# A two-layer decoder step on one core: the second layer's last three expert slots added to stored rows by DMA, and two slots' rows given to the next layer by one-hot products

## The chip, the cores and the metric

One NeuronCore of a Trainium2 chip. The metric is the device time of one execution in microseconds; the time before is the median of three runs. All positions in time below are microseconds from the start of the one profiled execution.

## The reference, cut to what matters

Two layers run over 512 prompt tokens and 64 sample tokens of width 1024. A layer adds a mixer (chunk MLP and differential attention) to x and then a mixture of experts, in which each token goes to the two best experts of its best group (4 groups of 4 experts):

```
def hier_moe(x, g2, r_g, r_e, w_gate, w_up, w_down):
    h = rmsnorm(x, g2).reshape(b * t, d)
    pg = softmax(h @ r_g);  gi = argmax(pg);  gw = max(pg)
    le_sel = (h @ r_e).reshape(-1, 4, 4)[:, gi]
    tw, ti = top_k(softmax(le_sel), 2);  tw = tw / sum(tw)
    gates = one_hot(gi * 4 + ti) * gw * tw
    a = silu(h @ w_gate) * (h @ w_up) * gates
    return a @ w_down          # summed over the experts

for l in range(2):
    x = x + merge_out(...)     # mixer
    x = x + hier_moe(x, ...)
```

The outputs are x of both token groups, and keys, values and normalised rows of each layer.

## The kernel before, in words

Tokens stand in five tiles of 128 rows (four of the prompt, one with the 64 sample rows, whose number is TP = 4); x is held in SBUF, [128, 5, 1024]. Each engine has its own program written out by hand, and semaphores with names order them: `full[u]` and `read[u]` say that a PSUM bank u was written or read, `landed` that a weight piece is there, `x_ready` that a tile of x is done.

The experts of a layer run as 13 slots of 128 rows (`SLOTS`, line 86); a slot belongs to one expert or is shared by two or three, and the experts are ordered by size while the kernel runs. For slot n POOL gathers rows by an indirect DMA, PE turns them, multiplies them with gate and up weights (`up`), turns the activations (`turn_act`) and multiplies with the down weights (`down`); ACT copies the result from PSUM to `y_sb` (`result`, line 1473), and POOL scatters its 128 rows into the DRAM tensor `y_rows` (`scatter`, line 651). A token has two rows there: its upper choice in the first 640 rows, its lower choice in the last 640. A choice of one of a group's first three experts lands in either half; the fourth experts (positions 12 to 15, slots 9 to 12) are always an upper choice. `LAST` is slot 10, the first slot whose first position is 12 or above; slots 10, 11 and 12 are the last three.

Weights come in pieces of 1 MB that SP issues in a fixed order (line 494) as buffers come free. In the second layer the third piece waits until the first layer's last upper rows have been loaded (`high_in`, line 470).

The end of a layer is this. When slots 8 and 9 have been scattered, ACT loads the lower rows of all tiles (line 1499), and DVE adds them to x with their gates behind the last slot's product (`add_low`, line 2127). After the last copy ACT waits for all scatters and loads the upper rows of all tiles (`load_high`, line 1535). DVE adds them tile by tile (lines 2186 to 2205). At the seam between the layers, tile 0 is added in two halves, and PE turns each half as soon as it is there (`turn_input`, line 757); until then PE runs 39 dummy products (`keep_busy`, line 755). In the second layer SP stores each tile when it is added (line 512), and the kernel ends when the stores have landed. Rows beyond the slots' capacity would go to extra slots (`extras`); the given input needs none.

Indices for the gather and scatter are products of one-hot matrices with row numbers (`index_rows`, line 1152; `index` on DVE, line 2006). At the start POOL writes zeros into the lower half of `y_rows` (line 571).

## Time and profile before

| what | value |
|---|---|
| median of 3 runs | 958.11 us (956.31 to 962.84) |
| profiled execution, its span | 959.0 us (no other time of it is given) |
| PE busy | 924.7 us, 96% |
| DVE, ACT, POOL busy | 396.8, 245.8, 190.9 us |
| DMA moved | 197.51 MB, 206 GB/s over the span |

Busy times are sums over the whole span; what a stage waits for is seen only in its own stretch. Two stretches matter here: the seam between the layers (about 460 to 490) and the tail (from 920 on). In a timeline row, the first number is the start, the second the duration (for several instructions in one row, from the first start to the last end), and what stands in brackets is the idle time before and what ended it. L715 and L713 are the lines of PE's helper, so all its products share them; a 128x128 by 512 product in f32 is two records. L656 is POOL's scatter; its duration is the time on POOL, and the rows land later.

### The profile page before, as it was taken

The page shows a single profiled execution, that of the slowest core. Times are in us where ns is not written, and L with a number is a line of the kernel's source. Part 1 is how long each engine was busy: PE and PEld are TensorE (multiplying, and loading weights), DVE is VectorE, ACT ScalarE, POOL GpSimd, SP SyncE. Part 2 cuts the span into 40 slices and gives each one's busy share as a digit, 9 for nine tenths or more (in the row PEclk, how much of TensorE's full clock was granted, in tenths as well). Part 3 has the DMA queues.
Part 4 walks back from the last instruction along what each step waited for, and adds up shares of the span by engine and source line. Part 5 has one row for each costly group of instructions (what it writes and reads, how often), then busy time and mean ns, then how long its engine had stood idle before and what let it go on. Part 6 is the DMA issues. An engine that isn't in the chain of part 4 may idle for free. (4 is left out here: it accounts for less than half of the span.)

```text
span 959.0 us, 13967 instructions
## 1 busy us (share of the span) xinstructions
PE 924.7 (96%) x5140; PEld 448.3 (47%) x5140; DVE 396.8 (41%) x1007; ACT 245.8 (26%) x493; POOL 190.9 (20%) x263
## 2 busy tenths in 40 slices
PE   9999999999999999999999999999999999999991
PEld 6444445556546443334544344455564464333330
DVE  2403225667547663111333122456764774511123
ACT  3211256552111021111131113765320012211110
POOL 2233201331200111111134032023220011111100
PEclk9999999999999999999999999999999999999996
DMA  9716003351017899998772150134210279999966
GB/s 334 290 46 273 2 1 138 89 176 45 23 45 265 319 410 399 401 403 352 263 268 65 36 239 1 55 109 156 84 45 22 114 267 411 414 386 403 423 236 231
DMA packets 39197, 197.51 MB, mean 206 GB/s; under 512 B 7096, under 2 KB 7224, under 8 KB 23248
## 3 DMA queue, kind: packets, MB, share of 16 engines
q1 hardware_dynamic: 19456, 136.03, 35.7%
q0 software_dynamic: 15312, 45.72, 13.8%
q10 hardware_dynamic: 4352, 14.76, 4.3%
q8 instruction: 45, 0.74, 0.3%
q14 instruction: 32, 0.26, 0.1%
HBM read 176.20 MB, written 28.84 MB: 214 GB/s over the span
## 5 line engine op out<-in xcount | busy, mean ns | idle before, releaser
L715 PE MATMUL ps<-ring,hT 128*128 128x512 f32 (+3 forms) x1312 | 397.1, 584 | 1.0 <-ACT ring L1406 0.6
L715 PEld LDWEIGHTS ps<-ring,hT 128*128 128x128 f32 (+2 forms) x1312 | 150.5, 152 | 197.2 <-issue 193.6
L715 PE MATMUL ps<-ring,cat 128*128 128x512 f32 (+2 forms) x560 | 181.8, 598 | 0.0
L715 PEld LDWEIGHTS ps<-ring,cat 128*128 128x128 f32 (+2 forms) x560 | 65.7, 157 | 81.0 <-issue 79.3
L2119 DVE TENSOR_TENSOR hT<-ps,par 128x512 f32<-128x512 f32 x52 | 33.7, 686 | 154.4 <-PE ps L713 149.4
L656 POOL DMA_INDIRECT y_rows<-hn,isca x26 | 27.0, 1039 | 230.7 <-ACT hn L1484 226.9
L535 POOL TENSOR_TENSOR st<-st,half 128x1 f32<-128x1 f32 (+3 forms) x60 | 63.5, 1058 | 11.0 <-POOL st L533 10.8
L533 POOL TENSOR_SCALAR st<-st 128x1 f32<-128x1 f32 (+3 forms) x60 | 16.0, 266 | 228.8 <-DVE st L1594 83.1
L1594 DVE TENSOR_REDUCE st<-sqj 128x8 f32<-128x512 f32 x20 | 13.5, 682 | 111.5 <-ACT sqj L1318 111.4
L715 PE MATMUL ps<-hT,ring 128*128 128x512 f32 x128 | 57.1, 599 | 0.7 <-DVE tmp L1651 0.7
L1484 ACT COPY hn<-ps 128x1024 f32<-128x1024 f32 x24 | 24.3, 1012 | 95.4 <-PE ps L715 95.4
L715 PE MATMUL ps<-kva,hT 128*32 128x512 f32 (+1 forms) x128 | 43.7, 596 | 0.0
L541 POOL DMA_DIRECT2D kc<-in_ck x32 | 24.6, 768 | 95.0 <-PE ps L715 71.7
L1390 ACT ACTIVATE ring<-ps,st 128x128 f32<-128x128 f32 (+3 forms) x64 | 33.2, 524 | 27.7 <-DVE st L1718 27.6
L1318 ACT ACTIVATE sqj<-ps,st 128x512 f32<-128x512 f32 (+1 forms) x20 | 13.7, 686 | 96.7 <-PE ps L715 90.1
L715 PEld LDWEIGHTS ps<-hT,ring 128*128 128x128 f32 x128 | 23.7, 190 | 29.9 <-issue 28.4
L648 POOL DMA_INDIRECT hT<-h_rows,igat x24 | 25.4, 1057 | 50.9 <-DVE isca L2017 45.4
L541 POOL DMA_DIRECT2D vc<-in_cv x32 | 17.6, 550 | 87.8 <-PE ps L715 71.9
L1467 ACT ACTIVATE cat<-ps 128x256 f32<-128x256 f32 x26 | 10.0, 384 | 96.9 <-PE ps L715 96.9
L1573 DVE TENSOR_TENSOR hT<-ps,g_sb 128x512 f32<-128x512 f32 x20 | 13.0, 688 | 48.6 <-PE ps L713 48.4
L715 PE MATMUL ps<-v,hT 128*32 128x512 f32 (+2 forms) x96 | 29.1, 596 | 1.8 <-SPq L167 1.8
L715 PE MATMUL ps<-kc,cat 128*32 128x512 f32 (+1 forms) x128 | 29.4, 596 | 0.0
(278 smaller groups left out, 1136.4 us busy)
## 6 DMA issues: line engine op xcount, KB each, us to landing
ring<-in_w SPq DMA_DIRECT2D x84, 1024.0 KB, 10.7
kc<-in_w SPq DMA_DIRECT2D x10, 1024.0 KB
vc<-in_w SPq DMA_DIRECT2D x10, 1024.0 KB
v<-in_w SPq DMA_DIRECT2D x10, 1024.0 KB
kva<-in_w SPq DMA_DIRECT2D x10, 1024.0 KB
kc<-in_ck POOLq DMA_DIRECT2D x32, 256.0 KB, 3.7
vc<-in_cv POOLq DMA_DIRECT2D x32, 256.0 KB, 3.3
h_rows<-qk ACTq DMA_DIRECT2D x10, 512.0 KB, 2.6
```

The lines of the kernel that those rows point to most:

```text
L533: nc.gpsimd.tensor_scalar(stat["ms"][at, 0:n], src, 1.0 / size, EPS, ALU.mult, ALU.add).then_inc(*pool_c.inc())
L535: nc.gpsimd.tensor_tensor(dst, stat["ms"][at, 0:n], half[at, 0:n], ALU.pow).then_inc(*pool_c.inc(*label))
L541: pool.dma_start(buffer(b % 2, g), view(d[table][bass.DynSlice(l * NPOOL + page, 1)])).then_inc(*arrived[b % 2].inc("kv", b, by=16))
L648: pool.indirect_dma_start(hs[:, b, :], None, h_rows, bass.IndirectOffsetOnAxis(index, 0), bounds_check=TOK - 1, oob_is_err=False).then_inc ...
L656: pool.indirect_dma_start(rows, bass.IndirectOffsetOnAxis(index, 0), y_sb[:, b, :], None, bounds_check=rows.shape[0] - 1, oob_is_err=False ...
L715: ins = pe.matmul(out, lhsT, rhs, start=start, stop=stop, skip_group_check=loose)
L1318: nc.scalar.activation(sqj[at, t % 2, :], bank(u)[at, :], ACT.Square, scale=stat["rs"][at, t:t + 1]).then_inc(*act_s.inc("sq", name, t))
L1390: ins = nc.scalar.activation(e_sb[:, n % 2, m, 0:(i + 1) * P], bank(f"S{n % 2}", m)[:, 0:(i + 1) * P], ACT.Exp, bias=stat["nb"][:, c:c + 1 ...
L1484: nc.scalar.copy(y_sb[:, b, :], ps[:, 6:8, :].rearrange("p a n -> p (a n)")).then_inc(*read["O"].inc("down", *key))
L1573: vec.tensor_tensor(hT[:, hf * HALF:(hf + 1) * HALF, t * P:(t + 1) * P], bank(f"T{hf}").rearrange("p (j t) -> p j t", j=HALF), g, ALU.mult ...
L1594: vec.tensor_reduce(stat["ssk"][:, 8 * t:8 * t + 8], groups(sqj[:, t % 2, :], 8, DK), AX.X, ALU.add).then_inc(*dve_s.inc("ss" + name, t))
L2119: vec.tensor_tensor(hsT[:, b, hf * HALF:(hf + 1) * HALF, :], bank(f"T{hf}").rearrange("p (j t) -> p j t", j=HALF), g, ALU.mult).then_inc(* ...
```

## The change

It does two things.

**Second layer.** The lower rows and the upper rows of slots 0 to 9 are loaded by SP together (`y_low` and `y_soon`), when slots 8 and 9 have been scattered. DVE adds both (`add_low`, `add_soon`): tiles 0 to 2 after the product of slot 11, tiles 3 and 4 after that of slot 12. SP stores each tile at once, into one output tensor `y`, which has three times 128 rows more than tokens. For slots 10, 11 and 12 PE and DVE make each row's gate (`slot_gates`, at slots 8 and 9; parts prepared in `direct_gates`), ACT multiplies it in when it copies the result, and POOL adds the 128 rows to `y` in DRAM by an indirect DMA with addition; rows of a slot that hold no token go to one of the additional rows. POOL's first such DMA waits until all five stores have landed.

**Seam.** When slot 10 has been scattered, ACT loads tile 0's upper rows (`first_rows`) before it copies the result of slot 11, and DVE adds them. The results of slots 11 and 12 are kept in SBUF (`y_kept`), and PE multiplies them with two one-hot matrices (`token_hot`) to get what tile 0 still lacks, in two halves, each two products; DVE adds the halves from PSUM. POOL scatters slots 11 and 12 only after `first_rows` has landed; ACT then loads the upper rows of tiles 1 to 4. The 39 dummy products become 4 before the four products and 2 behind them.

Besides, POOL writes one more blank of 128 rows at the start, and DVE computes `direct_gates` at slot 6 in both layers.

```diff
+        DIRECT = range(LAST, NSLOT)
+        GATES_AT = 8
+        y_soon = [ring[:, c, i * D:(i + 1) * D] for c in (1, 4) for i in range(2)] + [first_rows]
+        y_last = ring[:, 0, 0:D]
+        CARRIED = range(NSLOT - 2, NSLOT)
+        y_kept = [ring[:, 4, i * D:(i + 1) * D] for i in range(2)]
+        token_hot = [oS[:, 0:P], oS[:, 3 * P:4 * P]]
...
@@ SP
                         sp.wait_ge(*high_in[TP].at("high"))
+                        sp.wait_ge(*full["S1"].at("carried", 1))
...
+                if l == L - 1:
+                    for b in range(2):
+                        sp.wait_ge(*y_out[b].at("y", "m", last_slot(b, LAST)))
+                    for t in range(NT):
+                        sp.dma_start(y_low[0:n, t, :], y_rows[TOK + at:TOK + at + n, :])...
+                        sp.dma_start(y_soon[t][0:n, :], y_rows[at:at + n, :])...
+                    for t in range(NT):
+                        sp.wait_ge(x_ready.sem, L * NT + t + 1)
+                        sp.dma_start(d["y"][at:at + n, :], x[0:n, t, :]).then_inc(*stored.inc(by=16))
...
-            for t in range(NT):
-                n = NROW if t == TP else P
-                sp.wait_ge(x_ready.sem, L * NT + t + 1)
-                sp.dma_start(d["ys"] if t == TP else d["yp"][t * P:(t + 1) * P, :], x[0:n, t, :]).then_inc(*stored.inc(by=16))
             sp.wait_ge(stored.sem, stored.now())
+            for b in range(2):
+                sp.wait_ge(*y_out[b].at("y", "m", last_slot(b)))
...
@@ POOL
+                    pool.dma_start(y_rows[0:P, :], blank).then_inc(*blank_out.inc(by=16))
...
+                    if l == L - 1 and key[0] == "m" and key[1] in DIRECT:
+                        wait(stored.sem, NT * 16)
+                        j = DIRECT.index(key[1])
+                        src = y_last if key[1] == NSLOT - 1 else y_sb[:, b, :]
+                        pool.indirect_dma_start(d["y"], bass.IndirectOffsetOnAxis(iadd[:, j:j + 1], 0), src, None,
+                                                bounds_check=d["y"].shape[0] - 1, oob_is_err=True, compute_op=ALU.add)...
+                        return
+                    if l < L - 1 and key == ("m", CARRIED[0]):
+                        wait(*soon_first.at("soon"))
...
@@ PE
-                    keep_busy(39, "I")
+                    keep_busy(2, "I")
...
-                        pe.wait_ge(*dve_s.at("half"))
+                        pe.wait_ge(*read["S0"].at("carried", 0))
...
+                def slot_gates():
+                    pe.wait_ge(*dve_s.at("gate_parts"))
+                    claim("I")
+                    for j, s in enumerate(DIRECT):
+                        for t in range(NT):
+                            mm(bank("I")[:, j * 4:j * 4 + 3], onehot[:, s % 4, t, :], gate_parts[:, t, 0:3], ...)
...
+                if l < L - 1:
+                    keep_busy(4, "T0")
+                    pe.wait_ge(*dve_s.at("token_hot"))
+                    for c in range(2):
+                        u = f"S{c}"
+                        claim(u)
+                        for j, s in enumerate(CARRIED):
+                            if j == 0:
+                                pe.wait_ge(*read["O"].at("down", "m", s))
+                            else:
+                                pe.wait_ge(*read["JI"[c]].at("down", "m", s))
+                            mm(bank(u), token_hot[j], y_kept[j][:, c * W:(c + 1) * W], start=(j == 0), stop=(j == 1), ...)
...
@@ ACT
-                    if n == LAST + 1:
+                    if n == LAST + 1 and l < L - 1:
...
+                    if n == NSLOT - 1 and l < L - 1:
+                        act.wait_ge(*y_out[(CARRIED[0] - 1) % 2].at("y", "m", CARRIED[0] - 1))
+                        act.wait_ge(*y_out[(CARRIED[0] - 2) % 2].at("y", "m", CARRIED[0] - 2))
+                        act.dma_start(first_rows, y_rows[0:P, :]).then_inc(*soon_first.inc("soon", by=16))
                     if n >= 1:
                         result((n - 1) % 2, ("m", n - 1), n >= 3)
...
-                    for t in range(NT):
+                    for t in range(1, NT):
                         high_load(t)
...
@@ DVE
                     gated(n % 2, ("m", n))
+                    elif n >= LAST + 1:
+                        for t in (range(3) if n == LAST + 1 else range(3, NT)):
+                            add_low(t)
+                            add_soon(t)
...
+                    dve.wait_ge(*soon_first.at("soon"))
+                    link(vec.scalar_tensor_tensor(x[:, 0, :], first_rows, stat["soon"][:, 0:1], x[:, 0, :], ALU.mult, ALU.add))
...
+                            dve.wait_ge(*full[f"S{hf}"].at("carried", hf))
+                            vec.scalar_tensor_tensor(x[:, 0, cols], bank(f"S{hf}"), stat["gAB"][:, 0:1], x[:, 0, cols], ALU.mult, ALU.add)...
```

## Rows read from the trace of the kernel before

**Rows 1.** The page: span, and busy time of the engines.
```profile
span 959.0 us, 13967 instructions
PE 924.7 (96%) x5140; PEld 448.3 (47%) x5140; DVE 396.8 (41%) x1007; ACT 245.8 (26%) x493; POOL 190.9 (20%) x263
```

**Rows 2.** Windows of 10 us: stretch, length, busy time per engine, clock, DMA share, GB/s.
```profile
460.00:470.00 10.00, 8.62 (x54) 3.68 (x46) 6.75 (x6) 2.57 (x5) 2.69 (x2) 1.00 0.57 209
...
940.00:950.00 10.00, 0.00 (x0) 0.00 (x0) 2.57 (x2) 0.00 (x0) 0.34 (x1) 0.56 0.75 254
```

**Rows 3.** The chain of waits in the tail: start, us, what.
```profile
937.92 0.59 ACT hn L1482
...
939.36 3.51 DMA y_rows<-hn,isca
...
952.55 1.28 DVE x L2125
```

**Rows 4.** Timeline of PE at the seam.
```profile
468.79 9.21 PE L731 MATMUL ps<-c 128*128 128x128 f32 x78 [1.38 <-ACT hn L1482]
477.84 1.21 PE L713 MATMUL ps<-c,x 128*128 128x128 f32 x8
479.27 5.39 PE L715 MATMUL ps<-ring,hT 128*128 128x512 f32 x12 [0.22 <-issue]
484.50 1.04 PE L713 MATMUL ps<-c,x 128*128 128x128 f32 x8
```

**Rows 5.** Timeline of ACT, POOL and DVE at the seam.
```profile
463.74 1.01 ACT L1484 COPY hn<-ps 128x1024 f32<-128x1024 f32 x1 [1.51 <-PE ps L715]
...
466.61 0.58 ACT L1480 COPY hn<-ps 128x512 f32<-128x512 f32 x1 [1.85 <-DMA y_rows<-hn,isca]
...
469.00 0.98 POOL L656 DMA_INDIRECT y_rows<-hn,isca  x1 [1.57 <-issue]
...
472.97 2.58 ACTq L1517 DMA_DIRECT2D cat<-y_rows  x5
...
476.92 1.42 DVE L2195 SCALAR_TENSOR_TENSOR x<-cat,st,x 128x512 f32<-128x512 f32 x2 [8.67 <-DMA cat<-y_rows]
```

**Rows 6.** Timeline of the second layer's last slot and of the tail.
```profile
919.76 2.98 ACTq L1499 DMA_DIRECT2D qk<-y_rows  x5
...
930.97 6.55 DVE L2125 SCALAR_TENSOR_TENSOR x<-qk,st,x 128x1024 f32<-128x1024 f32 x5
...
931.96 0.44 PE L713 MATMUL ps<-c,cat 128*128 128x128 f32 x2
...
942.89 2.27 ACTq L1517 DMA_DIRECT2D cat<-y_rows  x5
...
946.26 2.61 DVE L2125 SCALAR_TENSOR_TENSOR x<-cat,st,x 128x1024 f32<-128x1024 f32 x2 [8.74 <-DMA cat<-y_rows]
...
955.05 0.53 SPq L512 DMA_DIRECT2D out_ys<-x  x1
```

**Rows 7.** Windows chosen for their DMA rate and clock, columns as in rows 2.
```profile
38.00:42.00 4.00, 3.38 (x18) 2.04 (x17) 3.33 (x10) 1.17 (x2) 0.36 (x1) 1.00 0.08 31
...
453.00:465.00 12.00, 12.00 (x55) 4.36 (x54) 4.19 (x4) 3.15 (x5) 0.98 (x1) 1.00 0.97 368
...
938.00:941.00 3.00, 0.00 (x0) 0.00 (x0) 0.00 (x0) 0.50 (x1) 0.98 (x1) 1.00 0.25 94
941.00:942.00 1.00, 0.00 (x0) 0.00 (x0) 0.00 (x0) 0.00 (x0) 0.00 (x0) 0.65 0.98 397
```

**Rows 8.** Second layer: index products, PE's wait, and DVE at slot 7.
```profile
L715 PE MATMUL ps<-rows_of,cat 128*128 128x4 bf16 x30 | 1.6, 166 | 0.0
...
PE ps L715 <- SPq L167: 1.8, 1, 1.8
...
857.42 1.29 DVE L2119 TENSOR_TENSOR hT<-ps,par 128x512 f32<-128x512 f32 x2 [10.27 <-PE ps L713]
```

**Rows 9.** DMA issues: line, count, KB each, median us from issue to landing.
```profile
out_ys<-x SPq DMA_DIRECT2D x1, 256.0 KB, 3.5
c<-in_c ACTq DMA_DIRECT2D x1, 64.0 KB, 1.9
```

More of the change, by code:

```diff
@@ L700, in first_extras, with add_sums @@
                     only_if(pool, n_extra > 1, lambda: first_extra(1), uncounted=hs_inx)
-                extras(pool, n_extra, move, start=first_extras, uncounted=[*hs_inx, *y_outx])
+                def add_sums():
+                    for b in range(2):
+                        wait(*y_out[b].at("y", "m", last_slot(b)))
+                    for t in range(NT):
+                        n, at = NROW if t == TP else P, PLACE[t] * P
+                        wait(*summed.at("sum", t))
+                        pool.dma_start(d["y"][at:at + n, :], x[0:n, t, :], accum_op=ALU.add).then_inc(*topped.inc("added", by=16))
+                extras(pool, n_extra, move, start=first_extras, done=add_sums if l == L - 1 else None, uncounted=[*hs_inx, *y_outx])
         ATT = [(i, h) for i in range(TP) for h in range(H)]
@@ L1166, in index_rows @@
                                    start=(t == 0), stop=(t == NT - 1), inc=full[u].inc("idx", g) if ends and at.stop == P else None)
+                def slot_gates():
+                    pe.wait_ge(*dve_s.at("gate_parts"))
+                    claim("I")
+                    for j, s in enumerate(DIRECT):
+                        for t in range(NT):
+                            mm(bank("I")[:, j * 4:j * 4 + 3], onehot[:, s % 4, t, :], gate_parts[:, t, 0:3], start=(t == 0), stop=(t == NT - 1),
+                               inc=full["I"].inc("gates") if (s == NSLOT - 1 and t == NT - 1) else None)
                 def turn_in(b, key, arrival):
@@ L2016, in index @@
                     dve.wait_ge(*read[u].at("idx", g))
+                    for s in GROUPS[g]:
+                        if l < L - 1 and s in CARRIED:
+                            vec.tensor_scalar(stat["row"][:, CARRIED.index(s):CARRIED.index(s) + 1], work[:, s - s0:s - s0 + 1], SKIP + 1.0, None, ALU.add)
+                        if l == L - 1 and s in DIRECT:
+                            vec.tensor_scalar(iadd[:, DIRECT.index(s):DIRECT.index(s) + 1], work[:, s - s0:s - s0 + 1], SKIP, c32[:, C_SINK][:, DIRECT.index(s):DIRECT.index(s) + 1], ALU.add, ALU.min)
                     vec.tensor_scalar(isca[:, s0:s0 + n], work[:, 4:4 + n], SKIP, None, ALU.add).then_inc(*dve_s.inc("idx", g))
@@ L2115, in in_turned, with slot_gates @@
+                def slot_gates():
+                    dve.wait_ge(*full["I"].at("gates"))
+                    n = len(DIRECT)
+                    vec.tensor_reduce(stat["hand"][:, 0:n], bank("I")[:, 0:4 * n].rearrange("p (s c) -> p s c", c=4)[:, :, 0:3], AX.X, ALU.add).then_inc(*read["I"].inc("gates"))
                 def in_turned(b, key, halves=(0, 1)):
@@ L2158, in _ @@
                         late_gates()
+                    if n == 6:
+                        direct_gates()
+                    if n == GATES_AT + 1 and l == L - 1:
+                        slot_gates()
                     if n in INDEX_AT:
@@ L2172, in slot, with sum_late @@
                     gated(b, (key, b))
+                def sum_late():
+                    dve.wait_ge(stored.sem, NT * 16)
+                    for t in range(NT):
+                        n = NROW if t == TP else P
+                        dve.wait_ge(*low_in[t].at("low"))
+                        dve.wait_ge(*high_in[t].at("high"))
+                        link(vec.tensor_scalar(x[0:n, t, :], y_low[0:n, t, :], stat["late"][0:n, t:t + 1], None, ALU.mult))
+                        vec.scalar_tensor_tensor(x[0:n, t, :], y_high[0:n, t, :], stat["rest"][0:n, t:t + 1], x[0:n, t, :], ALU.mult, ALU.add).then_inc(*summed.inc("sum", t))
                 def add_late():
@@ L2182, in extra_index @@
                         index(g)
-                extras(dve, n_extra, slot, done=add_late, start=extra_index)
+                extras(dve, n_extra, slot, done=add_late if l < L - 1 else sum_late, start=extra_index)
                 def add_high(t):
```

141 lines of the change are left out of this document (106 added, 35 removed).

## The prediction

> **What bounds the kernel now.** I read the page first: PE is busy 924.7 of 959.0 us [rows 1], so only two places can give much: where PE stands still, and where it does work that is none. The windows show both [rows 2]. From 460 to 470 PE is busy 8.62 of 10 us and then runs dummy products; from 940 on it does nothing, while DMA is at 0.75. The chain of waits gives the order of that tail [rows 3]: ACT copies the last slot's result (937.92), POOL scatters it into y_rows (939.36, landed 3.51 later); five loads bring all upper rows back from 942.89, DVE adds them, and x is stored until 958.55 (issue 955.05 [rows 6] plus 3.5 to landing [rows 9]). So 20.5 us pass after the last copy, all of it one DMA waiting for another. The timeline of the seam shows the same chain once more [rows 4, 5]: copy, scatter, load of tile 0 (issue 472.97), DVE's addition at 476.92, first product of the next layer at 479.27. The 9.21 us of dummies at 468.79 lie inside this wait. The granted clock is 1.00 throughout until PE stops.
>
> All times below are on the clock of the profiled execution. The page gives no time for it beside the span, 959.0, which is 0.9 above the median of the runs; 0.9 is taken off at the end.
>
> **Seam, step by step.** Tile 0 gets the rows of slots 0 to 10 by a load (first_rows) and those of slots 11 and 12 by one-hot products from SBUF.
> - ACT now waits for the scatter of slot 10 before result(11). That landing ended a wait at 466.6 in the trace [rows 5], and before it held only the last slot's copy. Issue of first_rows 0.5 (five issues took 2.58), result(11) 1.01, two half copies of 0.58: done at 468.1, 468.7 and 469.3. Before, result(11) stood at 463.74, so ACT is late, but nobody on PE asks yet: PE itself resumed only at 468.79, 1.38 after its last instruction.
> - PE: a dummy is 9.21/39 = 0.236, so 4 take 0.9 and end at 469.7. A product of 128x128 by 512 is two records of 5.39/12 = 0.45 [rows 4], so 0.9; four take 3.6, to 473.3, each after its copy. Two dummies more: 473.8. From the turn of tile 0 to the first product took 1.43 (477.84 to 479.27): 475.2. That is 4.0 earlier.
> - DVE: first_rows (512 KB) is bounded by 3.5 (a transfer of 256 KB [rows 9]) and 3.95 (472.97 to 476.92, one of five [rows 5]); I take 3.5, since it goes alone: 470.1. One addition of 1.28, then the end-of-layer branch, as PE's 1.38: 472.8. Two half additions of 0.71 (1.42 for two) end at 473.5 and 474.2. PE asks at 473.8 and 474.4, so the slack is 0.2 to 0.3 us.
> - POOL: scatter 11 has to wait for first_rows, since it writes rows that the load reads: 470.1 plus 0.85 (ACT's end to POOL's issue, 938.51 to 939.36 [rows 3]) is 471.0; scatter 12 follows 1.3 later (0.98 and a gap), 472.3, against 469.00. Landing 3.5 to 4.0 later (939.36 row; 469.00 to 472.97): 476.0. Behind it wait ACT's loads of tiles 1 to 4, and behind these SP's weight pieces. Tile 1 lands at 476.0 + 3.9 = 479.9 and is added by 481.2. PE, which started at 475.2, asks for tile 1 after 5.39, at 480.6, and waits 0.6. So the turn of tile 1 comes at 481.2 instead of 484.50: **3.3 us gained**. The tile after it lands 1.4 later, and PE asks for it 7 us later. What is late next is the load of tile 1; a microsecond more on first_rows costs one.
>
> **Second layer.** Five PE instructions per slot build the gates of three slots: 15 of the index form, which took 1.6/30 = 0.053 each [rows 8], 0.8 us. Later in this layer PE waits 1.8 us for the last weight piece (issued by SP, full queue) [rows 8], which should cover it; without that cover it is 0.8. I take 0.4. The 17 small DVE operations at n = 6 fall into idle time of 10.27 us before the next turn [rows 8]; nothing waits for them before n = 8. The sixth blank write (512 KB on POOL) falls into the start, where DMA is nearly free from 38 to 42 (0.08 [rows 7]) and PE waits for no load: nothing; 1.4 us if it stood ahead of a piece that PE waits for.
>
> **Tail.** SP starts ten loads when the scatters of slots 8 and 9 have landed: 919.76, when ACT's five loads started for the same landing [rows 6]. Behind this wait on SP stand only the stores, as all weight pieces are issued by then; ACT is rid of its five issues (2.98), which gains nothing, since its next copy waits for PE. These loads are 4.72 MB. Loads of this kind, with others, moved at 368 GB/s [rows 7], 1.42 per 512 KB; the first one in the tail took 3.37 (942.89 to 946.26 [rows 6]), so 1.95 ahead of the data. The third pair has landed at 919.76 + 1.95 + 6 x 1.42 = 930.2. DVE's six additions of 1.28 [rows 3] keep pace and end at 931.5; gated(12) stands behind them on DVE and ends at 931.9; PE's turn for it was at 931.96 [rows 6]. So the last slot is just not held. The other four additions follow: 937.1. The fifth store is issued there and lands 3.5 later, 940.6; by bytes (4.72 loaded and 2.36 stored at 368) it would be 940.9. I take 940.8. POOL's scatter of slot 10 waits for all five, and those of slots 11 and 12 stand behind it on POOL's queue, though their rows were ready by 938.5.
>
> So POOL issues at 941.7, 943.0 and 944.3. Now the unknown: the trace has no accumulating DMA. Plain, the last lands 3.51 later, at 947.8. Below this nothing lets it go. From the other side: 128 rows over 16 engines and three scatters are 24 rows on each engine, and if every row were a movement of its own without overlap, the nearest row is the smallest transfers' 1.9 us [rows 9], 45.6 us. I take the plain scatter's data time doubled, because each row is now fetched from y as well as from SBUF: 512 KB at 397 GB/s [rows 7] is 1.3, so 2.6 each, 7.9 from 943.0 to 950.9, and 0.8 to land: 951.7. It lies near the plain row, as the same rows move the same way. End 0.45 later, as from 958.55 to 959.0: 952.1, **6.9 us gained** (10.8 plain).
>
> Sum: 959.0 - 3.3 - 6.9 + 0.4 = 949.2, less 0.9: **948.3 us**.
>
> **Rivals.**
> - *The accumulation costs what a plain scatter does*: 3.9 less, 944.4. For it: rows of 4 KB flow at near the full rate. Against: twice the reads. The Trainium skill (DMA: Bandwidth & Descriptors, Anatomy of one DMA) gives 2.0 us plus bytes over 436 GB/s for a POOL-issued DMA, 3.2 for 512 KB where the row shows 3.51; an estimate from it with doubled bytes is 4.4, which would land the last at 948.7 and put the time near 945.3. Chance 0.25.
> - *Slower: rows do not overlap in the accumulation.* The place is the last 10 us, the price is per row. The gains are used up when the data phase lasts to 960.6 (959.0 + 3.3 - 0.4 - 1.25), 17.6 us or 0.73 a row against 0.165 plain; at 1.9 a row the time is about 986. For it: read, add and write of one row have to follow each other. Against: nothing says that different rows do. Chance 0.12.
> - *The seam gives nothing*: slot 10's landing or first_rows comes 3 us later, as in the last 3 us before 466.6, when the weights' two pieces and five loads share DMA. Scatters 11 and 12 and tile 1 move with it: 951.6. Chance 0.12.
> - *The new loads are slow and hold the last slot*: at the 254 GB/s of 940 to 950 [rows 2], the third pair lands at 934.1, gated(12) comes 3.9 late, loads and stores end at 949.6 and the tail at 960.9: 957.1. Chance 0.08.
> - *PE's clock falls at the seam*, since 33 dummies go. In the tail PE stands from 938.0 and the clock is still 1.00 until 941 and 0.65 in the microsecond after [rows 7]; the seam leaves it standing 1.4, as before. The Trainium skill (TensorE: Matmul & The Clock Gate, What's actually happening) says that throttled is the default and activity releases it. If it falls, 5.39 us of products take 10.8: 953.7 or more. Chance 0.03.
>
> **How the numbers follow.** The forecast has 0.40. One per cent, about what a measurement of this kernel tells from no change, is 9.6 us: the line is 948.5, right at the forecast. Faster by over 1%: the plain rival and a good half of the forecast (0.25), 0.50. Within: the rest of it, the seam, the loads and the clock, 0.38, of which I move 0.01 to the slower side for loads slower than priced. Slower: 0.13. The range goes from 941 (plain, seam at its 4.0, nothing for the gates, a little over) to 958 (slow loads): 0.8 inside, the unpipelined case outside.
>
> **What would show it.** Right: PE's first product of the second layer some 4 us after the end of four long products, and a turn of tile 1 held by a load; the store of the fifth tile landed 20 us after SP's first load; three POOL issues 1.3 apart behind it; the last landing 7 to 8 us after the last issue. Wrong: gated(12) starting after 932 (in old time), which holds the last slot; a last scatter of over 17 us; PE idle over 2 us or a clock under 1.00 at the seam; scatters 11 and 12 of the first layer issued after 474.

## The result and the profile after

The changed kernel takes 963.1 us (median of 20), the kernel before in the same comparisons 958.8: ratio 1.0036, 95% interval 1.0022 to 1.0049. It is slower by 0.4%, which is within one per cent; the time lies 5 us above the range of the prediction and 15 above its point. Its profiled execution has a span of 962.3 us and a time of 964.05.

The page, in place of [rows 1]:

```profile
span 962.3 us, 13931 instructions
PE 923.8 (96%) x5097; PEld 444.3 (46%) x5097; DVE 403.4 (42%) x1041; ACT 246.1 (26%) x493; POOL 192.0 (20%) x264
```

PE has less to do and the span is longer, so PE stands somewhere. The timeline of PE at the seam, in place of [rows 4] (L766 and L768 are the helper's lines now, L784 the dummies; L768 from `ring,oS` are the four long products):

```profile
464.90 0.27 PE L766 MATMUL ps<-c 128*128 128x128 f32 x1
471.20 2.08 PE L784 MATMUL ps<-c 128*128 128x128 f32 x8 [6.03 <-DVEq L168]
473.07 5.15 PE L768 MATMUL ps<-ring,oS 128*128 128x512 f32 x8
478.06 0.61 PE L784 MATMUL ps<-c 128*128 128x128 f32 x4
478.51 1.28 PE L766 MATMUL ps<-c,x 128*128 128x128 f32 x8
479.96 5.39 PE L768 MATMUL ps<-ring,hT 128*128 128x512 f32 x12 [0.17 <-issue]
485.18 1.04 PE L766 MATMUL ps<-c,x 128*128 128x128 f32 x8
```

PE stood for 6.03 us where before it stood 1.38, and it waited for line 168 of VectorE's queue, the place in a skipped branch (`only_if`) where the counts of the work that was not done are raised. A dummy's record then took 0.26 us (2.08 over 8) against 0.118 before, and a record of the four long products, which have two each, 0.64 (5.15 over 8) against 0.45. The windows of the same stretch say why (columns as in [rows 2]):

```profile
468.00:470.00 2.00, 0.00 (x0) 0.00 (x0) 1.28 (x1) 0.00 (x0) 0.94 (x1) 0.84 0.00 0
470.00:472.00 2.00, 0.80 (x3) 0.80 (x4) 0.00 (x0) 0.00 (x0) 1.18 (x2) 0.50 0.29 105
472.00:474.00 2.00, 2.00 (x8) 1.48 (x8) 0.00 (x0) 0.00 (x0) 0.00 (x0) 0.50 0.66 266
474.00:476.00 2.00, 2.00 (x4) 0.94 (x3) 0.00 (x0) 0.00 (x0) 0.00 (x0) 0.50 0.35 102
476.00:478.00 2.00, 2.00 (x5) 0.76 (x4) 0.75 (x1) 0.20 (x1) 0.41 (x1) 0.95 1.03 399
```

The clock fell to 0.50 (1.2 in place of 2.4 GHz) while PE stood, and was back at 0.95 in the stretch from 476, some five us after PE had resumed. The other engines at the seam, in place of [rows 5]:

```profile
466.13 0.60 ACT L1574 COPY ring<-ps 128x512 f32<-128x512 f32 x1
...
468.07 1.28 DVE L2323 SCALAR_TENSOR_TENSOR x<-ws,st,x 128x1024 f32<-128x1024 f32 x1 [1.19 <-DMA ws<-y_rows]
470.51 0.98 POOL L697 DMA_INDIRECT y_rows<-ring,isca  x1 [0.30 <-issue]
...
474.26 1.79 ACTq L1619 DMA_DIRECT2D cat<-y_rows  x4
```

All that the products read was there at 466.7 (466.13 and 0.60). VectorE added first_rows at 468.07 and only then came to its branch; line 168 was reached at 471.13.

The tail, in place of [rows 6], from its timeline (SP's first load, DVE's first addition, gated(12), PE's turn for the last slot, DVE's last addition, POOL's first and last accumulation):

```profile
923.00 0.34 SPq L520 DMA_DIRECT2D qk<-y_rows  x1
927.38 1.28 DVE L2264 SCALAR_TENSOR_TENSOR x<-qk,st,x 128x1024 f32<-128x1024 f32 x1 [3.89 <-DMA qk<-y_rows]
935.28 0.41 DVE L2277 TENSOR_TENSOR cat<-cat,ps 128x256 f32<-128x256 f32 x1
935.75 0.44 PE L766 MATMUL ps<-c,cat 128*128 128x128 f32 x2 [1.10 <-DVE cat L2277]
940.88 1.28 DVE L2273 SCALAR_TENSOR_TENSOR x<-ws,st,x 64x1024 f32<-64x1024 f32 x1
946.85 1.62 POOL L689 DMA_INDIRECT out_y<-hn,iadd  x1 [31.20 <-DVEq L168]
950.67 1.54 POOL L689 DMA_INDIRECT out_y<-ring,iadd  x1 [0.30 <-issue]
```

And its chain of waits, in place of [rows 3]:

```profile
927.43 10.85 DMA ring<-y_rows
...
942.19 3.73 DMA out_y<-x
...
949.38 2.82 POOLq L161
```

The chain says that POOL's first accumulation waited for the last store (942.19 and 3.73: landed at 945.9). The bracket in the timeline names VectorE's queue instead; in most of the kernels below the same bracket names the store.

The last step of the chain is one that no timeline shows: line 161 is the drain in the same skipped branch. Asked for by its line, the instruction is there, in the changed kernel once for each layer:

```profile
L161 POOLq DRAIN  x2: 6802/9544/12287, 470.1 to 949.4; - x2
```

It began at 949.4 and lasted 12.29 us, to 961.7; the span ends at 962.3. The data of the accumulations had stopped at 958, as two windows of the tail show:

```profile
952.00:956.00 4.00, 0.00 (x0) 0.00 (x0) 0.00 (x0) 0.00 (x0) 0.21 (x1) 0.50 1.07 190
...
958.00:959.00 1.00, 0.00 (x0) 0.00 (x0) 0.00 (x0) 0.00 (x0) 0.00 (x0) 0.50 0.03 4
```

**Where the time went.** Three stretches, each from instruction to instruction, so that they add up. Seam: from the start of the first layer's last product (467.14 before, 464.90 after) to the first product of the second layer. Layer: from there to POOL's issue of slot 9's scatter (911.14 and 914.65). Tail: from there to the end of the span.

| us | before | predicted | after |
|---|---|---|---|
| start to the first layer's last product | 467.14 | 467.14 | 464.90 |
| seam | 12.13 | 8.83 | 15.06 |
| layer | 431.87 | 432.27 | 434.69 |
| tail | 47.86 | 40.96 | 47.65 |
| span | 959.0 | 949.2 | 962.3 |

In the predicted seam of 8.83 the first product comes after 8.1, and some 0.7 is lost again behind it, by the late tile 1. The seam is 6.2 over its prediction and the tail 6.7; these two are the miss. The first row and most of the layer's 2.4 turned out to be chance: over all the executions below the first row lies between 464.9 and 468.0, and for the layer see the next table. A part of this layer's 2.4 is the clock of one stretch, 0.66 from 770 to 780. It was 1.00 there in the kernel before, but 0.83 in old_tail below, which has the old second layer, so the change did not bring it.

### The profile page after: what moved, and what is told of

Read it like the earlier page. It is cut to its first block, busy times and chain, and to the rows that moved or that the text cites. A ratio compares the mean times of both kernels' runs of the same rounds, so it can differ in the third digit from the quotient of the medians.

```text
span 962.3 us, 13931 instructions
## 1 busy us (share of the span) xinstructions
PE 923.8 (96%) x5097; PEld 444.3 (46%) x5097; DVE 403.4 (42%) x1041; ACT 246.1 (26%) x493; POOL 192.0 (20%) x264
## 4 chain that ended last, share of the span: by engine, by line
PE 85%; DMA 5%; DVE 3%; issue 2%; ACT 2%; SPq 0%; POOLq 0%; ACTq 0%; DVEq 0%; POOL 0%
PE ps L768 77%; PE ps L766 7%; DMA y_rows<-hn,isca 3%; PE ps L784 1%; DMA ring<-y_rows 1%; DMA hT<-h_rows,igat 0%; DMA out_y<-x 0%; DMA ws<-y_rows 0%; DVE hT L1675 0%; ACT hn L1581 0%; POOLq L161 0%; SPq L520 0%; DVE tmp L1753 0%; DVE tmp L1808 0%; DVE x L2273 0%
## 5 line engine op out<-in xcount | busy, mean ns | idle before, releaser
L768 PE MATMUL ps<-ring,hT 128*128 128x512 f32 (+3 forms) x1312 | 397.1, 584 | 1.0 <-ACT ring L1486 0.6
L768 PEld LDWEIGHTS ps<-ring,hT 128*128 128x128 f32 (+2 forms) x1312 | 150.5, 152 | 197.3 <-issue 193.8
L768 PE MATMUL ps<-ring,cat 128*128 128x512 f32 (+2 forms) x560 | 181.8, 598 | 0.0
L768 PEld LDWEIGHTS ps<-ring,cat 128*128 128x128 f32 (+2 forms) x560 | 65.7, 157 | 81.0 <-issue 79.3
L697 POOL DMA_INDIRECT y_rows<-hn,isca x21 | 21.2, 1011 | 194.8 <-ACT hn L1581 185.0
L562 POOL TENSOR_SCALAR st<-st 128x1 f32<-128x1 f32 (+3 forms) x60 | 15.1, 252 | 224.6 <-DVE st L1696 81.0
L768 PE MATMUL ps<-hT,ring 128*128 128x512 f32 x128 | 57.1, 599 | 0.7 <-DVE tmp L1753 0.7
L1581 ACT COPY hn<-ps 128x1024 f32<-128x1024 f32 x21 | 21.3, 1012 | 88.4 <-PE ps L768 88.4
L768 PE MATMUL ps<-kva,hT 128*32 128x512 f32 (+1 forms) x128 | 43.7, 596 | 0.0
L1470 ACT ACTIVATE ring<-ps,st 128x128 f32<-128x128 f32 (+3 forms) x64 | 33.2, 524 | 27.9 <-DVE st L1820 27.8
L768 PEld LDWEIGHTS ps<-hT,ring 128*128 128x128 f32 x128 | 23.7, 190 | 29.9 <-issue 28.4
L768 PE MATMUL ps<-v,hT 128*32 128x512 f32 (+2 forms) x96 | 29.1, 595 | 1.0 <-DMA ring<-in_w 1.0
L768 PE MATMUL ps<-kc,cat 128*32 128x512 f32 (+1 forms) x128 | 29.4, 596 | 0.0
```

The source lines that it names most:

```text
L562: nc.gpsimd.tensor_scalar(stat["ms"][at, 0:n], src, 1.0 / size, EPS, ALU.mult, ALU.add).then_inc(*pool_c.inc())
L697: pool.indirect_dma_start(rows, bass.IndirectOffsetOnAxis(index, 0), src, None, bounds_check=rows.shape[0] - 1, oob_is_err=False).then_inc ...
L768: ins = pe.matmul(out, lhsT, rhs, start=start, stop=stop, skip_group_check=loose)
L1470: ins = nc.scalar.activation(e_sb[:, n % 2, m, 0:(i + 1) * P], bank(f"S{n % 2}", m)[:, 0:(i + 1) * P], ACT.Exp, bias=stat["nb"][:, c:c + 1 ...
L1581: nc.scalar.copy(y_sb[:, b, :], ps[:, 6:8, :].rearrange("p a n -> p (a n)")).then_inc(*read["O"].inc("down", *key))
```

## The experiments

A ratio is to the kernel before on the same chip; "under the changed kernel" is the difference of the two ratios (1.0036 for the changed one) times 958.8 us, and has about 2 us of uncertainty on either side (3 for seam_banks and loads_first), so the stages of the traces carry much of the argument.

| kernel | us | ratio (interval) | seam | layer | tail |
|---|---|---|---|---|---|
| before | 958.8 | 1 | 12.1 | 431.9 | 47.9 |
| changed | 963.1 | 1.0036 (1.0022 to 1.0049) | 15.1 | 434.7 | 47.6 |
| old_seam | 961.9 | 1.0017 (0.9995 to 1.0040) | 12.6 | 433.9 | 49.4 |
| old_tail | 961.1 | 1.0017 (0.9998 to 1.0036) | 13.6 | 432.7 | 45.5 |
| seam_order | 960.5 | 0.9993 (0.9972 to 1.0013) | 12.8 | 432.8 | 48.1 |
| seam_dummies | 961.7 | 1.0019 (0.9999 to 1.0040) | 12.4 | 434.0 | 46.7 |
| seam_banks | 968.2 | 1.0077 (1.0047 to 1.0107) | 19.7 | 433.0 | 48.8 |
| tail_nodrain | 962.4 | 1.0022 (1.0002 to 1.0041) | 13.0 | 432.5 | 46.8 |
| loads_first | 967.1 | 1.0071 (1.0046 to 1.0097) | 14.0 | 432.4 | 50.1 |
| plain_rows | 958.2 | 0.9979 (0.9957 to 1.0001) | 14.8 | 433.0 | 43.1 |
| seam_early | 956.5 | 0.9973 (0.9961 to 0.9985) | 9.7 | 433.8 | 47.6 |
| early_old_tail | 956.5 | 0.9968 (0.9951 to 0.9986) | 8.0 | 433.6 | 45.8 |
| seam_both | 959.2 | 1.0002 (0.9985 to 1.0020) | 10.2 | 433.0 | 47.2 |
| sample_first | 957.9 | 0.9980 (0.9959 to 1.0001) | 8.6 | 433.9 | 47.7 |

The table shows the chance in one execution: the same changed seam took 15.1, 13.6, 13.0, 14.0 and 14.8 us (mean 14.1), and the same old tail 47.9, 45.5 and 45.8. The layer's mean is 433.4 in its changed form (eleven executions) and 432.7 in its old one (three).

**The two halves of the change, one at a time.** The seam of before with the changed tail (first diff, the core), and the reverse (second):

```diff
-                    keep_busy(2, "I")
+                    keep_busy(39, "I")
...
-                        pe.wait_ge(*read["S0"].at("carried", 0))
+                        pe.wait_ge(*dve_s.at("half"))
```

```diff
-                if l == L - 1:
...
-                        sp.dma_start(y_soon[t][0:n, :], y_rows[at:at + n, :])...
...
-                if n == GATES_AT and l == L - 1:
-                    slot_gates()
```

> The seam of before (load of tile 0's upper rows, 39 dummy products) with the changed second layer and tail. The theory is that the change lost its time in two places: 2.9 us at the seam (15.06 us from the last product of the first layer to the first of the second, against 12.13) and about 1 us where the second layer's last slot is held, while the new tail as a whole is only 0.5 us shorter than the old one. By it this kernel takes 2.9 us less than the changed one, about 960.2 us, some 1.4 us more than the kernel before, and its seam is 12.1 us long with a clock of 1.00. Rival: the seam costs more than itself, since the lower clock there also shifts the second layer's slower clock stretch (its routing stage took 18.8 us against 16.3); then 5.4 us less, 957.7. Second rival: all the loss is in the second layer and the tail, and the seam's 15 us are one execution's chance; then no difference from the changed kernel, 963.1.

> The changed seam with the second layer and the tail of before. By the theory the seam alone costs 2.9 us: about 961.7 us against 958.8 of the kernel before, with PE standing for 6 us and a granted clock of about 0.5 for 6 us at the seam, and a tail of 21.0 us from PE's end. Rival: the seam costs nothing by itself and the new tail costs all of the 4 us; then 958.8. The two kernels of this pair, taken together, should add up to the changed kernel: their two differences from the kernel before sum to 4.3 us.

Measured: 961.9 and 961.1 us, both 1.8 under the changed kernel and 1.6 over the one before. The two add up to 3.3, near the changed kernel's 3.5. The intervals separate neither kernel surely from the one before or from the changed one, but they leave no room for a gain of over 0.5 us by either half; 957.7 us for old_seam, the rival of a shifted clock stretch, lies outside its interval (958.3 to 962.6). The seam of old_tail was 13.6 us long in its profiled execution, with the clock down to 0.50 as well, so 2.9 was too much for a typical seam: the means give 14.1 against 12.4 (before and old_seam), 1.7 us.

**The order on VectorE.**

```diff
                     for t in LOW_AT[NSLOT - 1]:
                         add_low(t)
-                    dve.wait_ge(*soon_first.at("soon"))
-                    link(vec.scalar_tensor_tensor(x[:, 0, :], first_rows, ...))
...
                 extras(dve, n_extra, slot, ...)
+                if l < L - 1:
+                    dve.wait_ge(*soon_first.at("soon"))
+                    link(vec.scalar_tensor_tensor(x[:, 0, :], first_rows, ...))
```

> Changed kernel, one edit: VectorE adds first_rows to tile 0 behind its end-of-layer branch, not ahead of it. The theory: PE stood 6.0 us at the seam because the banks T0, S0 and S1 that it claims are released only in VectorE's branch, and VectorE came to it only after it had waited for first_rows (1.19) and added (1.28). By it PE's stand shrinks by 2.4 us to about 3.6, the first product of the second layer comes 2.4 us earlier if the clock still falls and up to 4.6 us earlier if it does not: 958.5 to 960.7 us. Rival: PE waits for the kept rows' copies or for the landing of first_rows, not for the branch; then its stand stays at 6 us and the time at 963.1.

Measured: 960.5 us, 4 under the changed kernel; PE's stand 4.50 us. The release in the branch is what PE waits for, as the theory says, but the branch came sooner by less than 2.4 us. The chain of waits of this kernel shows it:

```profile
467.80 0.07 DVEq L154
467.87 1.88 issue
469.75 0.06 DVEq L161
...
469.89 0.03 DVEq L168
...
469.96 1.70 PE ps L784 x8
```

Line 154 is the jump into the branch. It cost 1.88 us here; in the changed kernel, after VectorE had stood 1.19 us for first_rows, the same jump cost 0.53. In the kernel before it had cost some 2.8 (469.5 to 472.4, its lines 153 and 160). Why was not tried.

**The dummies on another bank.**

```diff
-                    keep_busy(4, "T0")
+                    keep_busy(20, "I")
```

> Changed kernel, one edit: the 4 dummy products ahead of the four long ones go to bank I and are 20, so that PE does not have to wait for VectorE's branch with them. The theory says that the fall of the clock to 0.50 is a cost of its own: with dummies from about 467 to 471.5 the clock stays at 1.00, the four products take 3.6 us in place of 5.15, and the first product of the second layer comes about 2.5 us earlier, although the banks S0 and S1 are released as late as before: 960.6 us. Rival: the clock falls all the same, or its fall is hidden by the wait for VectorE; then 963.1.

Measured: 961.7 us, 1.6 under the changed kernel, seam 12.4. From its timeline and windows:

```profile
470.72 3.50 PE L784 MATMUL ps<-c 128*128 128x128 f32 x29 [0.73 <-issue]
474.06 3.60 PE L768 MATMUL ps<-ring,oS 128*128 128x512 f32 x8
```

```profile
470.00:472.00 2.00, 1.28 (x11) 1.28 (x12) 0.34 (x1) 0.00 (x0) 1.64 (x2) 1.00 0.15 45
472.00:474.00 2.00, 2.00 (x20) 2.00 (x20) 0.00 (x0) 0.00 (x0) 0.48 (x1) 1.00 0.65 250
```

The clock stayed at 1.00, and the four products took 3.60 us, the 3.6 of the prediction. Twenty were too many: VectorE's branch was done at 472.1, before they ended at 474.

**Both together.** The two diffs above, with 9 dummies.

> Changed kernel with the two earlier edits of the seam together: VectorE adds first_rows behind its branch, and PE's dummies go to bank I and are 9. Alone, each made the seam some 1.5 us shorter than the mean of the changed one (12.8 and 12.4 us): with the first the clock still fell to 0.55, with the second the banks S0 and S1 came late. The theory: together the products start about 470 at a clock of 1.00, and the first product comes 10 to 10.5 us after the end of the first layer: 3.5 to 4 us less than the changed kernel, 959.5 us. Rival: the addition of first_rows, now behind the branch, which took 3.2 us there, is then what comes last; the seam stays at 12.5 us and the time at 961.5.

Measured: 959.2 us, 3.3 under the changed kernel, seam 10.2 us: as the theory had it, and level with the kernel before.

**Other banks for the halves.**

```diff
-                    keep_busy(2, "I")
+                    keep_busy(6, "O")
...
-                    keep_busy(4, "T0")
...
-                        u = f"S{c}"
+                        u = "JI"[c]
```

> Changed kernel, seam only: the halves for tile 0 go to the banks J and I, which ScalarE releases, in place of S0 and S1, which VectorE's branch releases; no dummies ahead of the four long products, 6 in place of 2 behind them. The theory: PE's 6.0 us stand and the fall of the clock come from one thing, the release in VectorE's branch (done at 471.1). By it PE starts the four products at about 467, the granted clock stays at 1.00, VectorE's two half additions follow its branch at about 471.2, and the first product comes near 473.4 in place of 479.96; the turn of tile 1, held by its load (issued 474.26, 3.5 to 4.0 us), comes at about 479.5 in place of 485.18. So 5 to 6 us less than the changed kernel: 957.5 us. Rival 1: first_rows and the scatters behind it hold tile 1 as late as before; then 1 to 2 us less. Rival 2: what is gained at the seam is lost later in the second layer, where weights come at a fixed pace; then 963.1.

Measured: 968.2 us, worse by about 4. Neither rival was this. Its timeline of PE:

```profile
476.72 6.25 PE L768 MATMUL ps<-ring,oS 128*128 128x512 f32 x8 [10.59 <-ACTq L168]
...
485.58 2.81 PE L768 MATMUL ps<-ring,hT 128*128 128x512 f32 x6 [0.39 <-issue]
```

The release moved from VectorE's branch to ScalarE's, and there the counts are raised behind `load_high`, which waits for the last scatter. So PE stood 10.59 us. It shows one thing: 5.6 us more of seam than the mean gave some 4 to 5 us more of time, and the layer behind it took 433.0, as ever, so the second layer does not absorb what the seam loses. The mended form raises the counts of J and O ahead of the loads:

```diff
         if not arrivals:
             eng.drain()
+        for c in early:
+            if after[c] != c.local:
+                eng.sem_inc(c.sem, after[c] - c.local)
+                c.local = after[c]
         if otherwise:
             otherwise()
...
-                extras(act, n_extra, slot, done=load_again, otherwise=...)
+                extras(act, n_extra, slot, done=load_again, early=[read["J"], read["O"]], otherwise=...)
```

> The kernel of the banks J and I once more, with one thing added: ScalarE's branch at the end of a layer raises the counts of J and O before it issues the loads of the upper rows, not behind them. In that kernel PE had stood 10.6 us, until ScalarE's branch, since there the count of J stood behind four loads that wait for the last scatter; the seam took 19.7 us and the time 5.0 us more than the changed kernel, so a microsecond of the seam is a microsecond of the time. The theory: with the release ahead of the loads PE stands under 2 us, the clock stays at 1.00, the four products run from about 467 to 471, VectorE's branch ends at about 471 and its half additions follow; the first product comes 8 to 9.5 us after the end of the first layer in place of 13.0 to 15.1 (five executions of the changed seam, mean 14.1). So 5 us less than the changed kernel, about 958 us. Rival: tile 1, whose load waits for the scatters of slots 11 and 12, holds PE after the first tile; then the turn of tile 1 comes 3 us or more after PE asks for it and the time is 960.5 us or more.

Measured: 956.5 us, ratio 0.9973 (0.9961 to 0.9985): 6 us under the changed kernel and faster than the one before. Its timeline of PE:

```profile
465.13 0.27 PE L770 MATMUL ps<-c 128*128 128x128 f32 x1
467.28 3.67 PE L772 MATMUL ps<-ring,oS 128*128 128x512 f32 x8 [1.87 <-ACTq L164]
470.78 1.50 PE L788 MATMUL ps<-c 128*128 128x128 f32 x12
473.31 1.37 PE L770 MATMUL ps<-c,x 128*128 128x128 f32 x8 [1.02 <-DVE x L2366]
474.85 5.39 PE L772 MATMUL ps<-ring,hT 128*128 128x512 f32 x12 [0.17 <-issue]
480.07 1.04 PE L770 MATMUL ps<-c,x 128*128 128x128 f32 x8
```

The first product comes 9.72 us after the last one of the first layer, at a clock of 1.00. The turn of tile 1 follows without a wait, so the rival (tile 1 late) does not decide. PE stood once behind it, 0.86 us at 483.69, for VectorE's copy of tile 1's turned rows, which stands behind the addition of tile 2.

**The mended seam with the old tail.** The two last diffs on old_tail.

> The same mended seam, with the second layer and the tail of the kernel before. From the issue of slot 9's scatter to the end the old tail took 47.9 and 45.5 us in two executions, the changed one 46.7 to 49.4 in five; from the first product of the second layer to that scatter the old form took 431.9 and 432.7, the changed one 432.4 to 434.7 in eight. The theory: the changed tail and its gates cost about 2 us and the mended seam gains 3 to 4 us on that of before; this kernel is then faster than both, about 955.5 us. Rival: the old tail is no better, and the gain of the seam is given back in the second layer; then 958 to 959.

Measured: 956.5 us, 0.9968 (0.9951 to 0.9986); seam 8.0 us. It too beats both kernels, but not seam_early: the two times are equal, where the stages of the traces made the changed layer and tail 2 us dearer. Whether the changed tail costs 2 us or nothing stays open; that it gains nothing does not.

**The tail without the drain.**

```diff
-        if not arrivals:
+        if not arrivals and drained:
             eng.drain()
...
-                extras(pool, n_extra, move, ...)
+                extras(pool, n_extra, move, ..., drained=l < L - 1)
```

> Changed kernel, one edit: GpSimd's branch at the end of the second layer has no drain. In the changed kernel that drain lasts from 949.4 to 961.7, 2.7 us after the last data of the accumulations moved, and the count that SyncE waits for at the end stands behind it; in the kernel before a drain of 6.1 us stood at 939.6 and lay beside the loads. The theory: 2.7 us of the end are this drain alone; without it the end comes about 0.5 us after the last landing, at 959.5, and the time is 2.5 us less, 960.6 us. Rival: the last landing itself is reported only at 961.7 and the drain merely ends with it; then 963.1.

Measured: 962.4 us, 1.3 under the changed kernel and within the uncertainty; from the last accumulation's issue to the end 11.0 us against 11.6. Neither side was right. Asked for the line of the program's end, and for what SyncE waited for last, the trace says:

```profile
L210 POOLq EVENT_SEMAPHORE  x2: 17/17/17, 958.4 to 958.5; - x2
L210 POOLq DRAIN  x1: 11927/11927/11927, 946.4 to 946.4; - x1
```

```profile
L545 SPq EVENT_SEMAPHORE  x1: 2926/2926/2926, 952.8 to 952.8; - x1
```

SyncE had its last landing at 952.8 + 2.9 = 955.7. But a drain stands at the end of every engine's program too, and GpSimd's lasted from 946.4 to 958.4, 2.7 us past that landing. The drain taken out had only stood ahead of it. In the kernel before, both of its drains in this branch are in the trace, and the prediction could have read them:

```profile
L160 POOLq DRAIN  x2: 6132/6218/6303, 469.3 to 939.6; - x2
```

The second began at 939.6 behind a scatter that landed at 942.9 [rows 3] and ended at about 945.8, some 3 us past it, under the loads of the upper rows. So the price was paid before as well, where it cost nothing. It is the price of having GpSimd's DMAs come last.

**Stores behind the loads.**

```diff
+                    sp.wait_ge(*soon_in[TP].at("soon"))
                     for t in range(NT):
                         sp.wait_ge(x_ready.sem, L * NT + t + 1)
```

> Changed kernel, one edit: SyncE stores no tile before the last of the ten loads has landed. The theory: the stores of tiles 0 to 2 share the DMA with the last loads (the last load took 10.9 us, at 230 GB/s for a stretch of 4 us), the tail hangs on the last addition and its store, so loads alone end earlier; VectorE's ten additions then set the pace, the last store lands about 1.5 us earlier, the last slot is held 0.5 us less: 961.6 us. Rival: the five stores then come in a heap behind the last addition and land as late or later; then 963.1 to 965.

Measured: 967.1 us, 3.4 worse than the changed kernel; tail 50.1. The loads were no faster without the stores: from slot 9's scatter to the end of the last addition 27.6 us against 27.5, and the stores then came in a heap (first accumulation issued 34.8 us after that scatter, against 32.2). The windows:

```profile
935.00:937.00 2.00, 2.00 (x18) 0.58 (x18) 1.25 (x1) 0.37 (x1) 0.00 (x0) 1.00 0.90 166
```

The DMA engines are 0.90 busy at 166 GB/s before the first store is issued at 939.15, in the last loads: the two of 64 rows, and the end of tile 3's, which lands at 937.9. So sharing with the stores was not what slowed the last loads. That it is the shape of 64 rows is a guess here, and the next kernel tries it.

**The sample tile first.** seam_early, with the order of loads, additions and stores changed.

```diff
+        ENDING = (TP, *range(TP))
...
-                    for t in range(NT):
+                    for t in ENDING:
```

> The kernel with the mended seam (956.5 us), one edit in its tail: the sample tile, of 64 rows, is loaded, added and stored first of the five, not last. In the kernel whose stores waited for the loads, the last loads were no earlier than with the stores beside them, and moved at 166 GB/s while the DMA engines were 0.90 busy; these were the two loads of 64 rows. The theory: loads of 64 rows keep the engines busy at half the rate, and at the end of the queue the last additions wait for them (about 2 us of VectorE's waits among its last four additions). With them first, the same bytes take as long, but VectorE starts sooner on 1.3 us additions and is not kept waiting at the end: the last store lands 1 to 1.5 us earlier, 955.3 us. Rival: the low rate is that of the queue's end, whatever stands there, or the last slot is held longer since the first three tiles take as long; then 956.5 us or more.

Measured: 957.9 us, 0.9980 (0.9959 to 1.0001), no different from seam_early. The slow stretch went along to the front, and the end ran at the full rate:

```profile
918.00:920.00 2.00, 2.00 (x6) 0.81 (x6) 0.00 (x0) 1.11 (x1) 0.00 (x0) 1.00 0.85 207
...
932.00:934.00 2.00, 2.00 (x6) 0.92 (x5) 1.97 (x2) 1.23 (x2) 0.00 (x0) 1.00 1.03 422
```

The reading of the 64-row loads holds: the last addition ended 26.1 us after slot 9's scatter in place of 27.4. The gain does not follow: the first accumulation was issued 31.5 us after that scatter in place of 31.9, since the last store, now of 128 rows, landed 4.5 us after its issue in place of 3.6.

**What the addition costs.** The three indirect DMAs of the tail without their addition.

```diff
-                                                bounds_check=..., oob_is_err=True, compute_op=ALU.add)
+                                                bounds_check=..., oob_is_err=True)
```

> Changed kernel, one edit that changes the output: the three indirect DMAs of the tail overwrite rows of y and do not add to them. It prices the addition. In the changed kernel an issue takes 1.6 us on GpSimd and the next comes 1.9 later, and from the last issue (950.67) to the last data 7.3 us pass at about 190 GB/s. The theory: the addition doubles the data time, so without it the issues come 1.3 apart and the last lands 3.6 us after its issue: the end comes 1.2 + 4.2 = 5.4 us earlier, 957.7 us. Rival: the rate is that of scattered rows in three transfers together whether they add or not, and the long way to the landing belongs to GpSimd's queue; then 1 us or less, 962.

Measured: 958.2 us, 5.5 under the changed kernel, as the theory had it. The timeline and a window, to set beside the 190 GB/s above:

```profile
946.10 1.00 POOL L689 DMA_INDIRECT out_y<-hn,iadd  x1 [31.98 <-DMA out_y<-x]
...
948.80 0.98 POOL L689 DMA_INDIRECT out_y<-ring,iadd  x1 [0.30 <-issue]
```

```profile
948.00:952.00 4.00, 0.00 (x0) 0.00 (x0) 0.00 (x0) 0.00 (x0) 1.47 (x2) 0.50 0.89 357
```

With the addition an issue takes 1.6 us on GpSimd in place of 1.0, three take 3.8 from first to last in place of 2.7, and the data moves at 190 GB/s in place of 357. From the last issue to the end it is 11.6 us against 7.4.

## Why the prediction was wrong

**The seam: the failed step is "so 4 take 0.9 and end at 469.7".** The prediction let PE resume 1.38 us after its last product, as before. Before, the dummies went to bank I, which ScalarE's last copy frees [rows 4]; the change put them on T0 and the halves on S0 and S1, whose counts VectorE raises in its end-of-layer branch, behind an addition that waits for first_rows. The prediction did count that branch, but only ahead of VectorE's half additions, not as what frees the banks of the products, and it priced it by PE's 1.38, a wait that ScalarE's copy ended [rows 4]. PE stood 4.4 to 6.0 us in the five executions with this seam. What the branch costs VectorE lay in the trace of before: the first of its counts there (line 167) is raised at 472.6, some 4.4 us behind VectorE's last addition (466.98 and 1.27) and 5.5 behind the start of the layer's last product; the prediction had the four dummies begin 1.7 behind that start. In the changed kernel line 168 came 1.8 behind the addition of first_rows.

**The clock, a rival at 0.03, came true**, for this very reason: the argument was that the seam leaves PE standing 1.4 us, as before. Its "1.00 throughout until PE stops" was not quite so either: from 300 to 310 the trace of before has 0.83. The Trainium skill (TensorE: Matmul & The Clock Gate, What's actually happening) says that the throttled state is the default and activity releases it; the trace agrees here, 0.50 after PE's stand and 0.95 some five us after it resumed. Its price is smaller than the 5.4 us of the rival, since the products that it hit were others: 1.6 us on the four products (5.15 against 3.60; 1.1 to 1.9 in the five executions) and about 1 on the four dummies ahead of them (2.08 against four times 0.236).

**All else at the seam was right.** first_rows took 3.59 us (464.38 to 467.97 in the chain of waits; predicted 3.5). POOL issued scatters 11 and 12 at 469.06 and 470.51; moved by the 2.24 us by which this first layer ended earlier, that is 471.3 and 472.8 (predicted 471.0 and 472.3). With the release mended, the first product came 9.7, 8.0 and 8.6 us after the last one of the first layer (seam_early, early_old_tail, sample_first; predicted 8.1) and the turn of tile 1 14.9, 13.2 and 13.8 us after it (predicted 14.1, before 17.4). So the mechanism gives its 3 us, once the banks are free in time; early_old_tail, which has this seam and the old second layer, is 3.1 us faster than the kernel before (1.3 to 4.7).

**The second layer was right**: 0.4 predicted, 0.6 between the means. The fifteen index products of the gates were 0.5 us of busy time.

**The tail: three terms were too small and one was missing.** In us after the issue of slot 9's scatter:

| | predicted | changed kernel | added here |
|---|---|---|---|
| loads start | 8.6 | 8.4 | -0.3 |
| last addition ends | 26.0 | 27.5 | 1.8 |
| POOL's first accumulation | 30.6 | 32.2 | 0.1 |
| POOL's last accumulation | 33.2 | 36.0 | 1.2 |
| last rows landed | 40.6 | 44.3 | 0.9 |
| end | 41.0 | 47.6 | 2.9 |

- "368 GB/s [rows 7]" for the loads: the two loads of 64 rows move at about half of that. The last slot was held too (gated(12) at 935.28, 1.1 us of PE), but not by these two: it stands behind the additions of tiles 0 to 2, and the first of them began 4.4 us after SP's first load in place of 3.4. PE is off the path in this tail: its last product ended at 941.8, five us before POOL's first accumulation.
- "1.3 later" for POOL's issues: with the addition 1.9.
- "I take the plain scatter's data time doubled": right. 1.57 MB at 190 GB/s is 8.3 us, against 7.9. The rival by the Trainium skill's formula (DMA: Bandwidth & Descriptors, Anatomy of one DMA), an estimate of 4.4 us for doubled bytes, is refuted: the last accumulation landed 8.3 us after its issue, with two others beside it, and 4.1 after it without the addition.
- "End 0.45 later, as from 958.55 to 959.0": that end was a store of SyncE. Here GpSimd's drain comes last, 2.7 us behind the landing. This is the missing term, and it lay in the trace of before.

The same steps in reverse say why the change could not gain much in the tail: it replaces a scatter, five loads and their additions by three accumulations at half the rate, with a drain that nothing covers. The profiled execution of before also flattered the change, since its tail of 47.9 was 2 us longer than the same tail in two other executions.

## What to carry to other kernels

When products move to other banks or earlier in time, ask for each bank who raises its count last and what stands ahead of that on its engine; a skipped branch is work too, and its releases should come ahead of any wait that they don't need. Fill a forced wait of PE with products on a bank that is really free, since the fall of the clock comes on top of the wait. What ends a program decides its price: read the drains by their lines, not in the timeline, before letting GpSimd's DMAs be the last to land.

## What was not expected of the hardware

- GpSimd's drain lasts until 2.7 to 3 us after its last DMA has landed (12.29, 11.93 and about 6.2 us in three places), whether it stands in a branch or at the end.
- An indirect DMA that adds moved 190 GB/s where the plain one moved 357, and its issue took 1.6 us on GpSimd in place of 1.0. These 1.6 us are not the transfer: the Trainium skill (Perfetto Trace Analysis, DMA Instruction — SWDGE (GPSIMD)) says that the profile's end of such an instruction is the end of writing its descriptors, and the trace agrees, with data moving for 6 us after the last one ended at 952.2.
- Stretches with loads of 64 rows had the DMA engines 0.85 to 0.90 busy at 166 to 207 GB/s, at the end of the queue and at its start, where one without them reached 422 at 1.03.
- The jump into a skipped branch cost VectorE 0.53 us in the changed kernel, 1.88 in seam_order and some 2.8 in the kernel before.
